# Transposing rotated queries and keys on VectorE instead of TensorE

## The reference

```python
for i in range(DEPTH):                       # DEPTH = 2
    hn = rms_norm(x, pre_norm_g[i])
    y = moba_mixer(hn, ...) if i % 2 == 0 else conformer_mixer(hn, ...)
    x = x + rms_norm(y, post_norm_g[i])

def moba_mixer(hn, w_in, w_out):
    q, k, v, z = jnp.split(hn @ w_in, 4, axis=-1)        # 16 heads of 128
    q, k, v = apply_rope(to_heads(q)), apply_rope(to_heads(k)), to_heads(v)
    o = moba_attention(q, k, v)
    return (o * jax.nn.silu(z)) @ w_out
```

## Time and profile before

| | |
|---|---|
| median of 3 runs | 864.7 us (863.1 to 865.91) |
| profiled execution | 864.29 us |
| its span | 862.3 us |
| mean granted TensorE clock | 0.998 of full speed |
| PE busy | 851.4 us, 99% |
| DVE busy | 573.7 us, 67% |
| ACT busy | 434.7 us, 50% |
| POOL busy | 332.8 us, 39% |
| DMA, mean over the span | 185 GB/s |

### The profile page before, as it was taken

One profiled execution on the slowest core, in us unless ns is written; L12 is line 12 of the kernel. 1 busy time (PEld: TensorE's weight loads), 2 busy tenths in 40 slices (PEclk: granted clock), 3 DMA queues, 4 the chain that ended last, 5 costly groups with the idle time before them and its releaser, 6 DMA issues.

```text
span 862.3 us, 12161 instructions
## 1 busy us (share of the span) xinstructions
PE 851.4 (99%) x4005; PEld 707.7 (82%) x4005; DVE 573.7 (67%) x951; ACT 434.7 (50%) x608; POOL 332.8 (39%) x169
## 2 busy tenths in 40 slices
PE   8999999999999999999999999999999999999996
PEld 6888888888888888888888888888888888888884
DVE  5656555564556455564555827999999999766555
ACT  6745354554445354454445575444454554474441
POOL 0342004400342004400000098888888879873000
PEclk9999999999999999999999999999999999999999
DMA  9965656645665656645655546555556556557532
GB/s 322 296 195 149 194 150 193 192 149 149 192 195 152 189 154 193 188 149 206 200 190 196 180 147 196 195 172 184 181 194 193 173 171 195 194 184 257 195 98 97
DMA packets 97782, 159.50 MB, mean 185 GB/s; under 512 B 3317, under 2 KB 38741, under 8 KB 97365
## 3 DMA queue, kind: packets, MB, share of 16 engines
q1 hardware_dynamic: 97156, 158.77, 57.7%
q10 hardware_dynamic: 592, 0.28, 0.1%
HBM read 156.94 MB, written 2.10 MB: 184 GB/s over the span
## 4 chain that ended last, share of the span: by engine, by line
PE 97%; issue 1%; DMA 1%; ACT 1%; DVE 0%; ACTq 0%; DVEq 0%; POOLq 0%; POOL 0%
PE acc L413 29%; PE acc L415 29%; PE acc L414 29%; PE X L423 3%; PE acc L399 1%; PE acc L401 1%; PE acc L400 1%; PE acc L481 1%; PE X L547 1%; PE acc L496 1%; DMA xrow<-in_x 1%; PE X L556 0%; PE X L541 0%; PE X L540 0%; PE X L557 0%
## 5 line engine op out<-in xcount | busy, mean ns | idle before, releaser
L785 ACT ACTIVATE w_hi<-raw 128x1024 fp32r<-128x1024 f32 x282 | 298.8, 1061 | 371.4 <-PE acc L415 371.4
L1082 DVE TENSOR_TENSOR w_lo<-raw,w_hi 128x1024 fp32r<-128x1024 f32 x182 | 242.3, 1333 | 223.8 <-ACT w_hi L785 223.4
L413 PE MATMUL acc<-w_hi,xT_hi 128*128 128x512 f32 x864 | 340.9, 395 | 0.3 <-DVE xT_lo L1101 0.3
L415 PE MATMUL acc<-w_hi,xT_lo 128*128 128x512 f32 x864 | 336.8, 390 | 0.0
L414 PE MATMUL acc<-w_lo,xT_hi 128*128 128x512 f32 x864 | 336.2, 389 | 0.0
L1485 POOL TENSOR_TENSOR w_lo<-raw,w_hi 128x1024 fp32r<-128x1024 f32 x100 | 243.2, 2440 | 49.0 <-ACT w_hi L785 48.9
L415 PEld LDWEIGHTS acc<-w_hi,xT_lo 128*128 128x128 f32 x864 | 162.2, 188 | 34.2
L413 PEld LDWEIGHTS acc<-w_hi,xT_hi 128*128 128x128 f32 x864 | 162.3, 188 | 32.7 <-DVE xT_lo L1101 0.5
L414 PEld LDWEIGHTS acc<-w_lo,xT_hi 128*128 128x128 f32 x864 | 162.4, 188 | 32.2
L1311 DVE SCALAR_TENSOR_TENSOR X<-u_pad,taps,X 128x256 f32<-128x256 f32 x464 | 182.7, 483 | 0.2
L1449 POOL TENSOR_TENSOR small<-small 128x1 f32<-128x1 f32 (+1 forms) x7 | 4.3, 617 | 233.7 <-DVE small L1257 126.9
(11 more groups left out here) (155 smaller groups left out, 704.6 us busy)
## 6 DMA issues: line engine op xcount, KB each, us to landing
raw<-in_w_in SPq DMA_DIRECT2D x78, 1024.0 KB, 5.3
raw<-in_w_in SPq DMA_DIRECT2D x66, 512.0 KB, 4.5
raw<-in_w_out SPq DMA_DIRECT2D x32, 1024.0 KB, 5.1
gpost<-in_post_g SPq DMA_DIRECT2D x2, 1024.0 KB, 4.8
raw<-in_w_in SPq DMA_DIRECT2D x4, 256.0 KB, 4.8
xrow<-in_x SPq DMA_DIRECT2D x2, 512.0 KB, 9.6
bout<-in_b_out SPq DMA_DIRECT2D x1, 1024.0 KB, 7.0
out<-xrow SPq DMA_DIRECT2D x4, 256.0 KB, 2.8
```

Of the source, the lines that this page charges most:

```text
L413: nc.tensor.matmul(a, hi[:, k, rows], w_hi[:, slot, i], start=(k == 0), stop=False)
L415: last = nc.tensor.matmul(a, lo[:, k, rows], w_hi[:, slot, i], start=False, stop=(k == KT - 1))
L785: nc.scalar.activation(w_hi[:, slot], raw[:, u % LOADS, 2 * half:2 * half + 2], ACT.Copy).then_inc(hi_ready[slot], 1)
L1082: nc.vector.tensor_tensor(lo_of(first, it, s), raw[:, u % LOADS, 2 * half:2 * half + 2], hi_of(first, it, s).bitcast(f32), ALU.subtract).t ...
```

## The change

The eight TensorE transposes of q and the eight of k go away in each group, with the four ACT copies that brought them to SBUF. DVE writes `qT` and `kT` itself, from `q_row` and `k_row`, with transposes in blocks of 32x32 from SBUF to SBUF. One operation reads 32 partitions (rows a*32 to a*32+31 of both row tiles) of 32 columns of each of the four heads, 256 elements per partition in eight blocks, and writes the 32 partitions b*32 and up of the target. 16 such operations (four a times four b) make up one of `qT`, `kT`.

Of the 16 for q, eight follow DVE's `low` of slice 15 and eight that of slice 16. The 16 for k follow in the same way behind slices 23 and 24. DVE waits for the rotation itself now, and before it overwrites `qT` of the group before, for the scores of that one. The scores stay behind TensorE's slice 22 and wait, as before, for `qT_ready` and `kT_ready`, which DVE now gives, and for the reads of the PSUM banks by the group before. POOL gets one wait between the rotations, for its own last addition to q_row.

```diff
@@ TensorE, group
-                    if s == 14:
-                        pe.wait_ge(rope_step, 6 * g + 3)
+                    if s == 22:
                         if first:
                             pe.wait_ge(vec_ready, 2)
                         else:
-                            pe.wait_ge(u_ready, g)
-                        pair_T(q_row, X[0], 0)
-                        pair_T(q_row, X[1], 2).then_inc(qT_done, 1)
-                    if s == 20:
-                        pe.wait_ge(rope_step, 6 * g + 6)
-                        if not first:
                             pe.wait_ge(ulo_ready, g)
-                        pair_T(k_row, X[2], 0)
-                        pair_T(k_row, X[3], 2).then_inc(kT_done, 1)
-                    if s == 22:
                         pe.wait_ge(qT_ready, g + 1)
                         pe.wait_ge(kT_ready, g + 1)
@@ ACT, group
-                    if s == 18:
-                        act.wait_ge(qT_done, g + 1)
-                        for b in range(2):
-                            last = nc.scalar.activation(qT[:, 2 * b:2 * b + 2], X[b][:], ACT.Copy)
-                        last.then_inc(qT_ready, 1)
-                    if s == 24:
-                        act.wait_ge(kT_done, g + 1)
-                        for b in range(2):
-                            last = nc.scalar.activation(kT[:, 2 * b:2 * b + 2], X[2 + b][:], ACT.Copy)
-                        last.then_inc(kT_ready, 1)
@@ DVE
+            def turn(dst, row, quadrants, done):
+                for a in quadrants:
+                    for b in range(4):
+                        last = nc.vector.transpose(
+                            dst[b * BLK:(b + 1) * BLK].rearrange("p h (m c) -> p m h c", m=MT)
+                            [:, :, :, a * BLK:(a + 1) * BLK],
+                            row[a * BLK:(a + 1) * BLK].rearrange("p m (h c) -> p m h c", h=G)
+                            [:, :, :, b * BLK:(b + 1) * BLK])
+                if a == 3:
+                    last.then_inc(done, 1)
@@ DVE, group, behind low(S_QKVZ, g, 32, s)
+                    if s in (15, 16):
+                        if s == 15:
+                            dve.wait_ge(rope_step, 6 * g + 3)
+                            if not first:
+                                dve.wait_ge(s_done, G * g)
+                        turn(qT, q_row, (0, 1) if s == 15 else (2, 3), qT_ready)
+                    if s in (23, 24):
+                        if s == 23:
+                            dve.wait_ge(rope_step, 6 * g + 6)
+                        turn(kT, k_row, (0, 1) if s == 23 else (2, 3), kT_ready)
@@ POOL
                 rotate(q_row, 4 * g + 1, 6 * g)
+                pool.wait_ge(rope_step, 6 * g + 3)
                 rotate(k_row, 4 * g + 2, 6 * g + 3)
```

More of the change, by code:

```diff
@@ L69 @@
              [slice(0, 768), slice(768, 1408), slice(1408, 1792), slice(1792, D)])
+BLK = 32
 DW_ROWS = TAPS * KT // 4
@@ L200, in build @@
         rope_step = sem("rope_step")
-        qT_done, kT_done = sem("qT_done"), sem("kT_done")
         qT_ready, kT_ready = sem("qT_ready"), sem("kT_ready")
```

## The result

The changed kernel takes 887.5 us (887.1 to 887.9, four runs) against 864.4 for the one before: ratio 1.026, 95% interval 1.025 to 1.028. I had said 874, with 866 to 885. The sign was right, the size was not: +23.2 us measured, +9.4 forecast.

What follows compares the result with a forecast made beforehand. TensorE was taken to bound the kernel (busy 851.4 of 862.3 us); 4 x 4.1 = 16.5 us of waits added less 7.1 removed gave +9.4, so 874, range 866 to 885, likeliest 871 to 877.

Steps and rivals of the forecast that it cites:

- Removed from TensorE, 7.1 us: Eight places behind slices 14 and 20, two per group, each a 0.88 us hole between products: 7.1 us off the path.
- ACT's copies, 0: Four 128x512 copies per group leave ACT; nobody on TensorE waited for them, so worth 0.
- p = 0.46: Start-to-start time of a DVE transpose in us, taken as not overlapping because partitions change; 0.35 to 0.40 if overlapping.
- The k transposes decide: TensorE waits before the scores behind slice 22 for DVE's k transposes: 16p - 3.24, about 4.1 us a group.
- The rotated keys are there by then: POOL's rotation of k ends before DVE's w_lo of slice 23 does, so DVE's new wait for POOL costs nothing.
- is level again before slice 23: Behind the q transposes DVE catches up by up to 1.5 us a slice and has no backlog left before slice 23.
- The q transposes are just hidden: w_lo of slice 17 is done at 154.85, needed at 155.12: 0.27 us left, hidden up to p = 0.477.
- The clock: Rival: TensorE's clock falls in the four new gaps of 4.1 us, 2.7 us a gap, up to +10.9, 885; 13%.
- 0.2 for restarting: Before the scores, about 0.2 us a group for the signal and a weight load no longer hidden, an estimate.
- rival 3: The clock falls in TensorE's new gaps before the scores: 885, or 879.5 where two of four are hit; 13%.

Runs made afterwards that it cites:

- last experiment: Changed kernel with q transposes four at a time behind DVE's slices 15 to 18 and scores behind TensorE's slice 24: 857.9 us, ratio 0.992.
- same-quadrant run: Changed kernel plus four more DVE transposes of the same size behind k's last eight, all from and to partitions 0 to 31, output unread: 889.9 us, one execution.
- Q alone: Changed kernel with only q transposed by DVE; k goes through TensorE and ACT as before: 872.7 us, ratio 1.009.
- k alone: Changed kernel with only k transposed by DVE; q goes through TensorE and ACT as before: 886.8 us, ratio 1.026.

## Why the prediction was wrong, step by step

- **Removed from TensorE, 7.1 us: right.** With the wait out of the way the median falls by 7.1 us in the last experiment (865.0 to 857.9), and the profiled execution by 7.3 from slice 0 to its end.
- **ACT's copies, 0: right as far as can be seen.** The 1.8 us that a group loses in the last experiment are all in the holes of the transposes.
- **p = 0.46: right**, 0.447. The choice between the two values that the rows allowed was the correct one, and the same-quadrant run bears out the first reason given, the other partitions; that a block has to be collected first was not tested.
- **"The k transposes decide", 16p - 3.24 a group: right as a mechanism, and in size when k goes alone** (3.91 by the formula, 3.86 measured). It alone would have given 4 x 3.86 - 7.1 = +8.3 us.
- **"The rotated keys are there by then": wrong, 4 x (5.5 - 3.86) = 6.5 us.** I took POOL's end, 166.64, from a trace in which DVE did one w_lo per 2.7 us, and let it stand in a schedule where five follow each other and each of POOL's products starts beside one. I had even used the other half of the same collision (w_lo 2.16 us long beside POOL) as a constant. That DVE "is level again before slice 23" was true, and the catching up was the damage. Q alone shows it without k.
- **"The q transposes are just hidden": right for TensorE's wait for w_lo** (w_lo of slice 17 ran from 159.07 and was done at 160.3, slice 17 started at about 160.8), wrong as a cost of 0.
- **The clock: a rival at 13%, and it came true in all four gaps, 8.0 us.** I had seen that TensorE would idle 4.1 us four times and that no row showed the clock behind such a stretch. The price per gap, 2.7 by guess, was 2.0; what failed is the chance. For a wait that the sum itself contained, the clock belonged in the sum. The Trainium skill (TensorE: Matmul & The Clock Gate, section "Why this matters for your kernels"), cited in rival 3, says that idle stretches of about this size send the clock down, and the four gaps here, of 5.3 to 5.6 us, agree.

Together: 9.4, less 1.1 for the two small sizes (p, and the 0.2 for restarting), plus 6.5 and 8.0, makes 22.8 of the 23.0 us by which the span grew. Either of the two missed terms alone would have left the time inside 866 to 885: with the clock held up it was 879.5, and without the late keys it would be 881 to 883 (864.7 + 8.3, and 8 to 10 for the clock by the change and by k alone; an estimate).

## What to carry to other kernels

When work moves to an engine with slack, ask what it does while it catches up: the compressed stretch collides with others, here DVE's w_lo with POOL, and the delay comes out on a third engine. A transfer of work off the bounding engine pays only if its result is still there when it is needed; move the consumer too, here by two slices, which turned +23 us into -5.5 (-7 with q spread as well). And a forecast wait of some microseconds on TensorE costs the wait and then the clock.

## What the runs showed of the hardware

- A DVE transpose of 32 partitions x 256 f32 elements lasts 436 ns, and such transposes start 0.447 us apart when the output quadrant changes each time; within one quadrant they last 390 ns and start 0.33 to 0.37 us apart.
- The granted clock fell from 2.4 to 1.2 GHz in each of the four gaps of 3.86 us (k alone) and of 5.29 to 5.55 (the change). Of the four stretches of 2.1 to 2.4 us (q alone) it fell behind two; of two that lasted 2.36 and 2.37 us, one had it and one didn't. With 20 products on a constant in the gap, 4.49 us of 5.55, it stayed up.
- A longer gap can hide more of the slow stretch: the scores took 5.11 us behind a gap of 3.86 and 4.59 behind one of 5.55, because 1.3 us of the low level lay in the first gap and 2.8 in the second.
- POOL's product of 128x256 takes 0.74 us when no w_lo of DVE is under way at its start, and up to 1.73 when one is. A w_lo, 1.23 us by itself, takes up to 2.16 us beside the rotation, and 3.22 when it starts behind POOL's large addition. Four transposes a group beside the rotation left POOL's times as they were and, at 0.75 us for two, were not slowed themselves.
